# Seven groups of adaLN projection columns weighted by VectorE and GpSimd, summed over partitions by TensorE

## The reference, cut to what matters

```
mod_l = silu(c)     @ w_ada[layer] + b_ada[layer]      # w_ada: (1024, 6 * 1024)
mod_c = silu(c_ctx) @ w_ada[layer] + b_ada[layer]
sh1, sc1, g1, sh2, sc2, g2 = split(mod, 6)
h = rms_norm(x) * (1 + sc1) + sh1;  parts = h @ w_in     # mLSTM, attention, conv, gates
x = x + g1 * (merge of the three branches) @ w_out
x = x + g2 * squared_relu_mlp(rms_norm(x) * (1 + sc2) + sh2)
```

## Time and profile before

| | us |
|---|---|
| median of 3 runs | 1922.48 (1922.08 to 1925.1) |
| the profiled execution | 1924.94 |
| its span | 1923.2 |
| TensorE matmul busy | 1876.0 |
| VectorE busy | 935.6 |
| ScalarE busy | 690.0 |
| GpSimd busy | 157.3 |

### The profile page before, as it was taken

How to read it: one execution, slowest core, us unless ns; L and a number is a source line. 1 busy time by engine, 2 the same in 40 slices (tenths; PEclk the granted TensorE clock), 3 DMA queues, 4 the chain that set the end, 5 groups by cost and what they waited for, 6 DMA issues and landing times.

```text
span 1923.2 us, 26643 instructions
## 1 busy us (share of the span) xinstructions
PE 1876.0 (98%) x11181; PEld 1608.0 (84%) x11181; DVE 935.6 (49%) x1370; ACT 690.0 (36%) x946; POOL 157.3 (8%) x155
## 2 busy tenths in 40 slices
PE   6999999999999999999999999999999999979998
PEld 4797788778778887878877788798988999969998
DVE  4525634544334343464333434644556556546664
ACT  3413543323222322343222222333543444434443
POOL 2101100002010100220000000201100110210000
PEclk9999999999999999999999999999999999989999
DMA  9221122221643344645334337222242355565562
GB/s 319 88 67 44 44 88 68 65 66 45 195 133 110 123 140 132 197 136 158 102 110 154 113 124 246 66 92 84 66 132 88 111 188 184 176 197 176 182 190 89
DMA packets 240855, 244.60 MB, mean 127 GB/s; under 512 B 6020, under 2 KB 239840, under 8 KB 240736
## 3 DMA queue, kind: packets, MB, share of 16 engines
q1 hardware_dynamic: 240432, 242.80, 39.8%
q10 hardware_dynamic: 304, 0.10, 0.0%
HBM read 241.83 MB, written 1.05 MB: 126 GB/s over the span
## 4 chain that ended last, share of the span: by engine, by line
PE 90%; DVE 4%; SPq 2%; ACT 1%; DMA 1%; issue 1%; POOL 0%; DVEq 0%; ACTq 0%; POOLq 0%
PE pp L961 19%; PE pp L965 19%; PE pp L962 19%; PE pp L968 4%; PE pp L969 4%; PE pp L970 4%; PE pc L1134 3%; PE pp L943 2%; PE pp L944 2%; PE pp L945 2%; PE pc L1186 2%; SPq L855 1%; PE pc L1224 1%; PE pc L1053 1%; PE pc L1201 1%
## 5 line engine op out<-in xcount | busy, mean ns | idle before, releaser
L961 PE MATMUL pp<-hH,wH 128*128 128x512 f32 (+1 forms) x1760 | 589.6, 345 | 4.5 <-DVEq L1770 3.1
L1636 DVE TENSOR_TENSOR wL<-raw,wH 128x1024 fp32r<-128x1024 f32 x358 | 465.6, 1341 | 250.1 <-ACT wH L1238 244.5
L962 PE MATMUL pp<-hH,wL 128*128 128x512 f32 (+1 forms) x1760 | 579.8, 340 | 0.0
L1238 ACT ACTIVATE wH<-raw 128x1024 fp32r<-128x1024 f32 x360 | 360.3, 1049 | 342.2 <-PE pp L970 218.7
L965 PE MATMUL pp<-hL,wH 128*128 128x512 f32 (+1 forms) x1760 | 455.9, 340 | 3.1 <-POOL hL L1574 2.3
L961 PEld LDWEIGHTS pp<-hH,wH 128*128 128x128 f32 x1760 | 334.0, 190 | 52.0 <-issue 12.7
L962 PEld LDWEIGHTS pp<-hH,wL 128*128 128x128 f32 x1760 | 334.2, 190 | 37.3 <-issue 1.7
L965 PEld LDWEIGHTS pp<-hL,wH 128*128 128x128 f32 x1760 | 303.3, 190 | 45.4 <-POOL hL L1574 8.5
L969 PE MATMUL pp<-yL,wH 128*128 128x512 f32 (+1 forms) x448 | 150.6, 336 | 0.0
L968 PE MATMUL pp<-yH,wH 128*128 128x512 f32 (+1 forms) x448 | 150.6, 336 | 0.0
L970 PE MATMUL pp<-yH,wL 128*128 128x512 f32 (+1 forms) x448 | 150.5, 336 | 0.0
(11 more groups left out here) (230 smaller groups left out, 1976.1 us busy)
## 6 DMA issues: line engine op xcount, KB each, us to landing
raw<-in_w_in SPq DMA_DIRECT2D x84, 1024.0 KB, 5.2
raw<-in_w_up SPq DMA_DIRECT2D x32, 1024.0 KB, 5.7
raw<-in_w_down SPq DMA_DIRECT2D x32, 1024.0 KB, 5.2
ada_T<-in_w_ada SPq DMA_DIRECT2D x18, 1024.0 KB, 7.9
ada_G<-in_w_ada SPq DMA_DIRECT2D x12, 1024.0 KB, 8.3
ada_Y<-in_w_ada SPq DMA_DIRECT2D x10, 1024.0 KB, 13.0
ada_H<-in_w_ada SPq DMA_DIRECT2D x8, 1024.0 KB, 9.5
raw<-in_w_proj_m SPq DMA_DIRECT2D x8, 1024.0 KB, 5.3
```

The lines of the kernel that those rows point to most:

```text
L961: pe.matmul(dsts[b], wh[b], hi[:, kt, ts_], start=first, stop=False)
L962: pe.matmul(dsts[b], wl[b], hi[:, kt, ts_], start=False, stop=False)
L1238: act.activation(wH[:, p % HIGH, a:a + KH, :], raw[:, p % RAW, a:a + KH, :], ACT.Copy).then_inc(wH_ready, 1)
L1636: dve.tensor_tensor(wL[:, p % RAW, ks, :], raw[:, p % RAW, ks, :], wH[:, p % HIGH, ks, :].bitcast(F32), ALU.subtract).then_inc(wL_ready, 1)
```

## The change

Groups are now of two kinds. Five stay as before (the first two, g2 of layer 0, sc2 and g2 of layer 1): 20 pieces. The seven others are 14 pairs of two pieces (1024 x 512, one DMA of 2 MB into home `W` or `G`). VectorE makes `acc[:, 0]`, the sum over the eight row blocks kt of w times silu(c) (a tensor_scalar, then seven scalar_tensor_tensor of 128 x 512, each chained to the one before). For the ten pairs whose context vector is read, GpSimd makes `acc[:, 1]` with silu(c_ctx): a product into `acc_t` and an addition into `acc[:, 1]` apart, 8 and 7 instructions of 128 x 512, each waiting for the one before. TensorE then sums over partitions with four matmuls whose stationary operand is a column of ones (`adasum`), one step of four column groups. The work of a pair comes in two or three portions after consecutive panels, and its `adasum` two panels after the last portion.

The plan: no pieces between panels. Pairs 0 to 5 (layer 0: g1, sh2, sc2) stand at layer 0's branch end, four panels apart; pairs 6 to 13 (layer 1: sh1, sc1, g1, sh2) in layer 0's MLP. Around the norms stand 4 pieces each: 2, 1, 1. The pieces of layer 1's second norm come from `W0`, `W1` (loaded at the branch end) and `Y0`, `Y1` (loaded during `wo`), no longer from `G0`, `G1`. The four pieces of layer 1's first norm all lie in `H0` to `H3`, and ScalarE's first write of hH waits for the fourth of them.

```diff
-        homes += ["T0", "T1"] * 6  ... (and the homes of the other groups)
+    for l, m, kind, v in ((0, 2, "sum", 2), (0, 3, "sum", 2), (0, 4, "sum", 2), (0, 5, "pe", 2), (1, 0, "sum", 2),
+                          (1, 1, "sum", 2), (1, 2, "sum", 1), (1, 3, "sum", 1), (1, 4, "pe", 2), (1, 5, "pe", 2)):
+        groups.append(dict(kind=kind, v=v, pieces=[(l, m, c) for c in range(NC)]))
+    homes += ["Y0", "Y1", "Y2", "Y3", "H0", "H1", "H2", "H3", "W0", "W1", "Y0", "Y1"]
...
+    def pair(n, load, sums):
+        later(load, "pairload", n=n)
+        each = KT // len(sums) + (KT % len(sums) > 0)
+        for i, at in enumerate(sums):
+            later(at, "weighted", n=n, kts=(i * each, min(KT, (i + 1) * each)))
+        later(sums[-1] + 2, "adasum", n=n, g=PAIRS[n]["group"])
+        if PAIRS[n]["j"]:
+            row_turn(sums[-1] + 2, PAIRS[n]["group"])
...
+            for n in range(FIRST_PAIRS):
+                at = count["panel"] + 4 * n
+                pair(n, at + 3, [at + 2, at + 3, at + 4])
+        else:
+            for i in range(2):
+                later(count["panel"] + 6 + 2 * i, "adaload", a=FILL_N2[l] + i)
...
+        for i in range(4 if l == 0 else 2):
+            later(count["panel"] + 3 + (i if l == 0 else 2 * i), "adaload", a=FILL_N2[l] + i + (0 if l == 0 else 2))
...
-        ada(4 if l == 0 else 2)
+        ada(2)
         step("squares", l, n=2, j=NC - 1)
         step("mean", l, n=2)
-        ada(2 if l == 0 else 1)
-        spread_apply(l, 2, 2 if l == 0 else 1)
+        ada()
+        if l == 0:
+            at = count["panel"]
+            for n, load, sums in ((0, 0, (1, 2, 3)), (1, 4, (5, 6, 7)), (2, 6, (9, 10, 11)), (3, 10, (13, 14, 15)),
+                                  (4, 14, (17, 18)), (5, 18, (20, 21)), (6, 21, (23, 24)), (7, 24, (26, 27))):
+                pair(FIRST_PAIRS + n, at + load, [at + i for i in sums])
+            for i in range(NC):
+                later(at + 31, "adaload", a=FILL_N1 + i)
+        spread_apply(l, 2, 1)
...
 # SyncE
-                    elif home in ("G0", "G1"):
-                        sp.wait_ge(h_ready, h_no[0 if a < FILL_3 else 1, "m", NC - 1] + 1)
+                    if home[0] == "W":
+                        pair_read(sp, len(PAIRS) - 1)
+                        sp.wait_ge(y_ready, y_no[1, "a", NC - 1] + 1)
                     elif home[0] == "Y":
+                        sp.wait_ge(panel_done, panel_no("proj", l, NC - 1, 2) + 1)
+            def load_pair(n):
+                q = PAIRS[n]
+                if same_pair[n]:
+                    pair_read(sp, same_pair[n][-1])
...
 # TensorE
+                elif k == "adasum":
+                    n, j = st["n"], PAIRS[st["n"]]["j"]
...
+                    pair_read(pe, n)
+                    for q in range(4):
+                        v, i = (q // 2 if PAIRS[n]["v"] == 2 else 0), q % 2
+                        last = pe.matmul(b[32 * q:32 * q + 32, 0:PC], ones_wide[:, 1 - j:33 - j], acc[:, v, i * PC:(i + 1) * PC],
+                                         start=j == 0, stop=j == 1, tile_position=(0, 32 * q))
...
 # GpSimd
+                elif k == "weighted" and PAIRS[st["n"]]["v"] == 2:
...
+                    for kt in range(a, e):
+                        to = acc[:, 1, :] if kt == 0 else acc_t[:, :]
+                        i = pool.tensor_scalar(to, src[:, kt, :], c2[:, kt, 1:2], None, ALU.mult)
+                        i.then_inc(acc1_chain if kt == 0 else acc1_step, 1)
+                        if kt:
+                            pool.wait_ge(acc1_step, (KT - 1) * sum(PAIRS[p_]["v"] == 2 for p_ in range(n)) + kt)
+                            i = pool.tensor_tensor(acc[:, 1, :], acc[:, 1, :], acc_t[:, :], ALU.add)
+                            i.then_inc(acc1_chain, 1)
+                        n_acc += 1
+                        pool.wait_ge(acc1_chain, n_acc)
...
 # VectorE
+                elif k == "weighted":
...
+                    if a == 0:
+                        acc_free(dve, n)
+                        dve.wait_ge(s_pair[q["home"]], 16 * (len(same_pair[n]) + 1))
+                    for kt in range(a, e):
+                        if kt == 0:
+                            i = dve.tensor_scalar(acc[:, 0, :], src[:, kt, :], c2[:, kt, 0:1], None, ALU.mult)
+                        else:
+                            i = dve.scalar_tensor_tensor(out=acc[:, 0, :], in0=src[:, kt, :], scalar=c2[:, kt, 0:1],
+                                                         in1=acc[:, 0, :], op0=ALU.mult, op1=ALU.add)
...
 # ScalarE, apply of layer 1
-                        ada_finished(act, FILL_2 + 3)
+                        ada_finished(act, FILL_N1 + NC - 1)
```

More of the change, by code:

```diff
@@ L91, in make_constants @@
             row_sum[p, p % 32] = 1.0
-    return np.concatenate([ident, row_sum, rot, np.cos(ang), np.sin(ang), sel.reshape(P, 32), one_row],
+    pair_row = np.zeros((P, 8), np.float32)
+    for v in range(2):
+        for piece in range(2):
+            for j in range(2):
+                pair_row[32 * (2 * v + piece) + j, 2 * (2 * j + piece) + v] = 1.0
+    return np.concatenate([ident, row_sum, rot, np.cos(ang), np.sin(ang), sel.reshape(P, 32), one_row, pair_row],
                           axis=1).astype(np.float32)
@@ L194, in step, with later, row_turn @@
         plan.append(dict(k=k, l=l, **kw))
+    def later(at, k, **kw):
+        owed.append((at, lambda: step(k, 0, **kw)))
+        owed.sort(key=lambda q: q[0])
+    def row_turn(at, g):
+        for wait, k in ((1, "adarow"), (2, "adaturn"), (2, "modulation")):
+            later(at + wait, k, g=g)
     def ada(n=1):
@@ L201, in ada @@
             count["ada"] += 1
[L202 to L206, removed]
+            step("ada", 0, a=a, g=g)
+            if a % NC == NC - 1 and a >= 2 * NC:
+                row_turn(count["panel"], g)
+    def pair(n, load, sums):
[6 more added lines that the diff above has]
+            row_turn(sums[-1] + 2, PAIRS[n]["group"])
     def ada_end(g):
@@ L373, in make_plan @@
             settle()
-            ada(4)
+            ada(2)
         step("squares", l + 1, n=1, j=NC - 1)
@@ L382, in make_plan @@
     step("final", DEPTH)
-    assert count["ada"] == ADAS and not owed
+    assert count["ada"] == len(ADA) and not owed
     p = 0
@@ L610, in trunk @@
         s_ada = {name: sem("ada_loaded_" + name) for name in ada_home}
+        s_pair = {name: sem("ada_pair_loaded_" + name) for name in pair_w}
+        acc_ready = sem("ada_pair_weighted")
+        acc1_step = sem("ada_pair_context_product")
+        acc1_chain = sem("ada_pair_context_weighted")
+        acc_used = sem("ada_pair_summed")
+        ones_ready = sem("ones_wide_ready")
         s_tables = sem("tables_loaded")
@@ L734, in ada_finished, with acc_free, pair_read @@
                 eng.wait_ge(ada_done, sum(ADA[q]["i"] != NC - 1 for q in range(a + 1)))
[L736 to L748, removed]
-                free_at = max(free_at, panel_no("wo", 1, 0) + 3 + (a - FILL_3) // 2)
-            return min(free_at, ada_at[a] + 2)
+        def acc_free(eng, n):
+            if n and PAIRS[n - 1]["j"]:
+                bk, un = pair_bank[n - 1]
+                eng.wait_ge(full[bk], un + 1)
+            elif n:
+                eng.wait_ge(acc_used, n // 2 + 1)
+        def pair_read(eng, n):
+            eng.wait_ge(acc_ready, n + 1)
+            if PAIRS[n]["v"] == 2:
+                eng.wait_ge(acc1_chain, KT * sum(PAIRS[q]["v"] == 2 for q in range(n + 1)))
         qk_order = [st["j"] for st in PLAN if st["k"] == "qrot" and st["l"] == 0]
@@ L869, in _ @@
             load_panel(0)
-            for a in range(NC, FIRST_ADA):
+            for a in range(NC, 2 * NC):
                 load_ada(a)
@@ L890, in _ @@
                 p = st["p"]
-                while next_ada < ADAS and ada_load_at(next_ada) <= p:
-                    load_ada(next_ada)
-                    next_ada += 1
                 if p >= 2:
@@ L1059, in _ @@
                         last.then_inc(ada_done, 1)
+                elif k == "adasum":
+                    n, j = st["n"], PAIRS[st["n"]]["j"]
+                    b = claim(u[0]) if j == 0 else pc[:, u[0][0], :]
+                    if n == 0:
+                        pe.wait_ge(ones_ready, 3)
+                    pair_read(pe, n)
[3 more added lines that the diff above has]
+                                         start=j == 0, stop=j == 1, tile_position=(0, 32 * q))
+                    if j == 1:
+                        filled(last, u[0])
+                    else:
+                        last.then_inc(acc_used, 1)
                 elif k == "adaturn":
                     b = claim(u[0])
+                    which = pair_row if ADA_GROUPS[st["g"]]["kind"] == "sum" else row_sum
                     for i in range(NB):
-                        last = pe.matmul(b[:, PC + 8 * i:PC + 8 * (i + 1)], ada_rows[:, st["g"] % 2, i * P:(i + 1) * P], row_sum,
```

(1 more changed line is left out.)

125 lines of the change are left out of this document (77 added, 48 removed).

## The result

The changed kernel takes 1909.69 us (median of 4, 1908.38 to 1912.88) against 1923.79 (4 runs in the same comparison): ratio 0.9927, 95% interval [0.9908, 0.9946], 14.1 us less. I had forecast 1899.4 (23.1 less than before), the forecast's own range 1892 to 1906 and 1891 to 1913 for 8 in 10. The profiled execution has a span of 1908.5 us.

The account below looks back on a forecast made before the run. TensorE bounds the kernel (98% busy), except at layer 1's `wo` gap. Terms -14.5 - 0.9 + 0.3 - 10 + 2 = -23.1 us from 1924.9 give 1901.8 profiled, 1899.4 median; own range 1892 to 1906, 8-in-10 range 1891 to 1913.

Parts of the forecast that it names:

- Pieces out, `adasum` in: TensorE between panels: 21 pieces removed save 25.4 us, 14 `adasum` cost 10.9 us; net -14.5 us (-8.5 to -19.4).
- Nothing charged: SyncE's panel loads behind pairs: wait about 6 us into a panel, panel lands some 18 us late, no cost.
- a product of 0.7 us: GpSimd's 128 x 512 product in a pair: taken as 0.7 us, bounds 0.29 and 1.29; 14.6 us a pair.
- my own list: Signs of being wrong: TensorE waiting for `wL` or y in layer 0's MLP, product above 1.4 us, 8.9 us gap staying.
- harm begins after about 30 us: Panel loads behind pairs: a panel is wanted after 11 us and its lateness harms only after about 30.
- VectorE and GpSimd: Layer MLPs and branch end: VectorE stands still while GpSimd runs, delaying splits or y; charged +2 us, 0 to 8.
- The norms: Fewer pieces around norms: layer 0's second norm -0.9 us; layer 1's first norm +0.3 us, 1.1 if slow.
- rival 4: TensorE's clock falls after longer idle at two norms: +4 us, 1903; counted with the forecast's chance of 0.62.
- The gap in `wo`: Layer 1's `wo` and following norm: earlier loads remove SyncE's 11.0 us wait and TensorE's delays; -10 us (0 to -12).
- Rival 1: Layer 1's gap stays, its place taken by earlier loads or x-update splits; only -13.1 us, 1909.4; chance 0.2.
- Rival 2: `adasum` costs a whole piece and VectorE's waits reach TensorE now and then: -11 us, 1911; chance 0.1.
- Rival 3: GpSimd's product takes 2.4 us, a pair 28 us, VectorE stands through it: slower, 1941 us; chance 0.05.

Follow-up runs that it names:

- e2: Changed kernel with the loads of pairs placed later in SyncE's order (branch end +5 instead of +3 panels, later in the MLP): 1904.84 us, ratio 0.9904 to the kernel before.
- e6: Changed kernel with e2, e4 and e5 together and the fourth piece of layer 1's first norm in G0 instead of H3: 1898.29 us, ratio 0.9856.
- e3: Changed kernel without seven of eight GpSimd products per pair, raw weights added instead (context sums not the reference's): 1906.96 us, ratio 0.9918.
- e4: Changed kernel with GpSimd's share, the context sums, given to VectorE: 1904.43 us, ratio 0.9904 to the kernel before.
- e7: As e6, but with the context sums left on GpSimd: 1897.67 us, ratio 0.9863 to the kernel before.
- e5: Changed kernel with the row copy ahead of a pair's portion on VectorE where both fall behind the same panel: 1902.23 us, ratio 0.988.
- e8: As e6, plus six steps of zero-column matmuls filling TensorE's wait ahead of `mean` at two norms: 1895.11 us, ratio 0.9846.
- e1: Kernel before with only layer 1's second-norm pieces moved from G0, G1 to T0, T1 and their loads re-placed: 1912.52 us, ratio 0.9945.

## Why the prediction was right and where it was wrong

The wide range held the time and the sign was right; the value was 10 us too low, outside the forecast's own 1892 to 1906, and the gain does not lie where I put it. That it fell inside the wide range is partly luck: the first half gave 14 us less than its terms, and layer 1 gave 3.6 us more, of which 1.4 lie in a row that the change leaves alone.

- **Pieces out, `adasum` in (-14.5).** Right in price: 0.77 us against 0.78, and 345.5 in e2, 359.3 in e6 against 345.9 and 359.0 from my terms. In the changed kernel itself it did not arrive, and TensorE was busy for 336.9 of the 340 us from 480 to 820, for which I had named all of them.
- **"Nothing charged" for the loads.** This step failed first. I had SyncE wait about 6 us into a panel for the earlier pair; it waited up to 33.6 us. The cause is the mis-sized term before it: a product of 0.7 us, with 1.29 as the upper bound. It is 1.56 at the least and 2.0 in the median, and by my own list, which says that I am wrong with a product above 1.4 us, this part of the prediction fails. An addition of two tensors was no bound for a product with one. The claim that harm begins after about 30 us was near: waits of SyncE of up to 20.2 us (e3, e4) left TensorE alone, 33.6 us did not, and e2 shows that it cost 5 us.
- **VectorE and GpSimd (+2, 0 to 8).** The mechanism was right, VectorE stands still behind GpSimd; its cost to TensorE by late weights or y was at most 1 us (e7). The harm came in a place that I did not look at, the order of a row copy and a portion behind the same panel, 4.1 us of wait and 3 of slow clock (gone in e5, which is 6.3 us shorter there). I had written that copies and turns stay 12, and counted them as equal for that.
- **The norms (-0.9, +0.3).** Measured -0.3 and +1.6. I held two fewer pieces before `mean` to be free, since TensorE waits there. The longer wait is followed by a longer time at half clock: rival 4, which I had described but not put into the sum. e8 shows what the slow clock behind these waits costs in e6, 2.6 us at each norm. Part of that was there before: from `mean` to the first panel it took 7.7 and 6.8 us before, 7.4 and 8.4 after, 5.2 and 5.3 in e8.
- **The gap in `wo` (-10).** Right, and 2.2 us too small: `wo` gave 4.8 of 4.7 and the way to `mean` 5.7 of 5.4, but the way from `mean` to `up` shrank by 1.8 us as well, since the clock had not fallen there. With the clock as it was in e1, e7 and e8 that part is 1.1.
- **Rivals.** Rival 1's number, 1909.4, is the measured one, but it is refuted: its gap closed. Rival 2's price for `adasum` is refuted; its other half, that VectorE's waits reach TensorE, came true at one place, the turn. Rival 3 had the right condition, a product above what I gave it (its 1.4 us was passed, and a pair took the 28 us that it names), and the wrong path: VectorE, where the path ran over SyncE.

## What to carry to other kernels

When work is moved off the bound engine, look first at who waits for the engine that takes it over, SyncE above all: a queue that waits for a reader delays everything issued behind it, and here it cost nothing to ask for that load a panel or two later. Small copies that the bound engine waits for go ahead of long optional portions in each engine's order. And work that fills a wait of TensorE is not always free to remove: here the idle time returned in the clock of what followed.

## What was not expected of the hardware

- GpSimd's tensor_scalar of 128 x 512 with a scalar per partition took 1.563 us at least, its tensor_tensor addition of the same shape 1.277. The Trainium skill ("GPSIMD Engine Reference", Engine selection) calls one-input work roughly line rate; here the measurement decides: 3.05 ns a column for one input and 2.5 for two. VectorE took 0.483 us for the same product in e4, where GpSimd had no portions.
- Behind a wait of 4.10 us TensorE ran at half clock for 6 us although it was busy throughout (0.50 from 866 to 870). Behind a wait of 3.16 us the piece at 1209.72 and the one at 1213.59 both took 1.93 us. A wait of 1.31 us did not tell alone what followed: behind the one at 1706.43 no piece was slow, behind those of e1, e7 and e8 the second one was.
- GpSimd's product of the first row block took up to 3.6 us beside VectorE's split, more than twice its own time: the exclusion works both ways. VectorE's own product of the first row block, which I had left out of the rule as it reads one tensor, took 1.49 us at 861.18 against 0.483 in e4.
